# Two pairs per loop turn on TensorE in the attention stage of a fused two-block kernel

## The reference, cut to what matters

```python
s = jnp.einsum('bhrcd,bhrjkd->bhrcjk', qg, kg) + bias[None]
s = jnp.where(col_mask[:, None, :], s, -jnp.inf)
p = jax.nn.softmax(s.reshape(B, NA_HEADS, rows, GRID_W, kh * GRID_W), axis=-1).reshape(s.shape)
o = jnp.einsum('bhrcjk,bhrjkd->bhrcd', p, vg)
na_out = neighbourhood_attention(na_q, na_k, na_v, rpb) * jax.nn.silu(na_z)
...
return jnp.concatenate([na_out, ml_out], axis=-1) @ w_out
```

## Time and profile before

| what | value |
|---|---|
| median of 3 runs | 1884.34 us (1883.26 to 1884.55) |
| span of the profiled execution | 1883.3 us |
| granted TensorE clock, mean | 0.999 |
| PE busy | 1865.6 us, 99% of the span |
| DVE, ACT, POOL busy | 982.4, 618.3, 552.5 us (52%, 33%, 29%) |
| gate of pair 1 to the end of the last values matmuls | 1451.3 to 1628.4 us |

### The profile page before, as it was taken

The page is one execution under the profiler, slowest core; times in us unless marked ns, Lnnn a source line. Parts: engine busy times, 40 slices in busy tenths (PEclk is TensorE's granted clock), DMA queues, the critical chain, the costliest instruction groups (busy, mean ns, idle before and its releaser), DMA issues.

```text
span 1883.3 us, 26698 instructions
## 1 busy us (share of the span) xinstructions
PE 1865.6 (99%) x10035; PEld 1540.4 (82%) x10035; DVE 982.4 (52%) x2117; ACT 618.3 (33%) x1317; POOL 552.5 (29%) x925
## 2 busy tenths in 40 slices
PE   9999999999999999999999999999999999999998
PEld 8888878888888888888888787888887777788886
DVE  6556565775666433114777322223213777776665
ACT  7321111233444432101222202221114667655552
POOL 2112222233642222110110000222314777544442
PEclk9999999999999999999999999999999999999999
DMA  6223142366897745312221123665563776867663
GB/s 197 95 79 119 62 128 81 104 184 235 306 266 252 235 168 162 101 50 84 74 78 68 53 62 116 211 211 171 168 220 105 243 232 224 271 219 241 230 229 112
DMA packets 236365, 303.55 MB, mean 161 GB/s; under 512 B 41414, under 2 KB 161126, under 8 KB 236204
## 3 DMA queue, kind: packets, MB, share of 16 engines
q1 hardware_dynamic: 205724, 215.84, 37.4%
q0 software_dynamic: 23600, 77.61, 11.4%
q10 hardware_dynamic: 6912, 8.39, 1.2%
HBM read 194.71 MB, written 107.54 MB: 160 GB/s over the span
## 4 chain that ended last, share of the span: by engine, by line
PE 94%; DVE 2%; DMA 2%; issue 1%; ACT 1%; POOL 0%; SPq 0%; POOLq 0%; DVEq 0%; ACTq 0%
PE banks L145 25%; PE banks L147 25%; PE banks L146 25%; PE banks L2106 3%; PE banks L2069 3%; PE banks L2088 3%; PE banks L2704 2%; PE banks L2706 1%; PE banks L2397 1%; DMA iraw<-in_w_in 1%; PE banks L2089 1%; PE banks L2674 1%; PE banks L234 1%; PE banks L1109 1%; PE banks L1741 0%
## 5 line engine op out<-in xcount | busy, mean ns | idle before, releaser
L145 PE MATMUL banks<-hT,wu 128*128 128x512 f32 (+1 forms) x528 | 204.6, 387 | 1.1 <-DVE wu L512 0.6
L147 PE MATMUL banks<-hT,wu 128*128 128x512 f32 (+1 forms) x528 | 202.3, 383 | 0.0
L146 PE MATMUL banks<-hT,wu 128*128 128x512 f32 (+1 forms) x528 | 202.2, 383 | 0.0
L145 PE MATMUL banks<-iT,wub 128*128 128x512 f32 x384 | 151.2, 394 | 0.0
L145 PE MATMUL banks<-iT,wua 128*128 128x512 f32 x384 | 150.8, 393 | 0.0
L145 PE MATMUL banks<-wub,iT 128*128 128x512 f32 x384 | 150.6, 392 | 0.0
L147 PE MATMUL banks<-iT,wub 128*128 128x512 f32 x384 | 149.7, 390 | 0.0
L147 PE MATMUL banks<-iT,wua 128*128 128x512 f32 x384 | 149.5, 389 | 0.0
L146 PE MATMUL banks<-wub,iT 128*128 128x512 f32 x384 | 149.5, 389 | 0.0
L147 PE MATMUL banks<-wub,iT 128*128 128x512 f32 x384 | 149.5, 389 | 0.0
L146 PE MATMUL banks<-iT,wua 128*128 128x512 f32 x384 | 149.5, 389 | 0.0
(11 more groups left out here) (293 smaller groups left out, 4116.3 us busy)
## 6 DMA issues: line engine op xcount, KB each, us to landing
iraw<-in_w_in SPq DMA_DIRECT2D x36, 512.0 KB, 4.4
wa<-in_w_ada SPq DMA_DIRECT2D x48, 256.0 KB
yT<-sg POOLq DMA_DIRECT2D x32, 256.0 KB, 3.1
oraw<-yT SPq DMA_DIRECT2D x32, 256.0 KB, 4.8
xr<-in_x SPq DMA_DIRECT2D x16, 512.0 KB, 4.4
h<-h POOLq DMA_DIRECT2D x16, 512.0 KB, 4.3
hT<-tr POOLq DMA_DIRECT2D x16, 512.0 KB, 5.1
tws<-wg SPq DMA_DIRECT2D x16, 512.0 KB, 5.1
```

Source lines behind the costliest of these rows:

```text
L145: e.matmul(ps, lh, rh, start=first, stop=False)
L146: e.matmul(ps, lh, rl, start=False, stop=False)
L147: return e.matmul(ps, ll, rh, start=False, stop=last)
```

## The change

PE's loop and DVE's loop take steps of two (p = 0, 2, ..., 66). With q = p-2, an even pair, a turn of PE's loop is now: turn(q); scores(q+3) and scores(q+4) together; the tail's early work; turn(q+1); values(q-1) and values(q) together. A turn of DVE's loop is: invert(q+1), lower(q+2), copy(q); invert(q+2), lower(q+3), copy(q+1); then gate(q-1) and gate(q). ACT, POOL and SP keep their loops. The values of even and odd pairs go to two banks up to pair 53; from pair 54 all go to one, since the tail's scores need the other. The tail's first scores move from p = 57 to p = 58 and wait for gate 53 (`o_out.ge(54)`); its first numerators move from p = 63 to p = 64. The bodies of the turn, the values, the copy and the gate become functions with the same waits and instructions, but that the values wait for the last pair of their own bank.

```diff
-        self.pS, self.pT, self.pO = self.last[0:4], self.last[4:6], self.last[6]
+        self.pS, self.pT = self.last[0:4], self.last[4:6]
+
+        self.pO = [self.last[7] if q % 2 and q < 54 else self.last[6] for q in range(self.NP)]
...
     def dve(self, e, w, tail):
-        for p in range(self.NP + 3):
-            q = p - 1
-            if 1 <= q < self.NP:
-                self.invert(e, w, q)
-            if 2 <= p < self.NP:
-                self.lower(e, w, p)
-            tail.between_dve(e, w, p)
...
+        for p in range(0, self.NP + 3, 2):
+            for x in range(2):
+                if 1 <= p + x - 1 < self.NP:
+                    self.invert(e, w, p + x - 1)
+                if 2 <= p + x < self.NP:
+                    self.lower(e, w, p + x)
+                tail.between_dve(e, w, p + x)
+                self.copied(e, w, p + x - 2)
+            for x in range(2):
+                self.weighed(e, w, p + x - 3)
+                tail.early_dve(e, w, p + x)
...
+    def product(self, e, w, q):
+
+        if 0 <= q < self.NP:
+            hp, _, a = self.pairs[q]
+            nb, g0 = self.blocks(q), self.window(q)[0] // 4
+            w.wait_ge(*self.pt_dve.ge(q + 1))
+            w.wait_ge(*self.pt_act.ge(q + 1))
+            w.wait_ge(*self.vm_in[hp % 2].ge(2 * (hp // 2 + 1)))
+            w.wait_ge(*self.v_in[q % 4].ge(q // 4 + 1))
+            before = max((x for x in range(q) if self.pO[x] is self.pO[q]), default=None)
+            if before is not None:
+                w.wait_ge(*self.o_out.ge(before + 1))
...
     def pe(self, e, w, tail):
         w.wait_ge(*self.proj.row_step.ge(48))
-        for p in range(self.NP + 3):
-            if 1 <= p and p + 1 < self.NP:
-                self.scores(e, w, p + 1)
...
+        for p in range(0, self.NP + 3, 2):
+            self.turn(e, w, p - 2)
+            for x in (p + 1, p + 2):
+                if 2 <= x < self.NP:
+                    self.scores(e, w, x)
             tail.early_pe(e, w, p)
+            self.turn(e, w, p - 1)
+            self.product(e, w, p - 3)
+            self.product(e, w, p - 2)
...
     def early_pe(self, e, w, p):
-        if p == 57:
-
-            w.wait_ge(*self.att.proj.row_step.ge(48))
+        if p == 58:
+
+            w.wait_ge(*self.att.o_out.ge(54))
             self.scores(e, w, 0)
-        if p == 63:
+        if p == 64:
 
             w.wait_ge(*self.att.s_out.ge(128))
             self.numerators(e, w, 0)
-        if p == 64:
             self.scores(e, w, 1)
             self.product_n(e, w, 0, 0)
```

More of the change, by code:

```diff
@@ L1976, in invert @@
         e.reciprocal(self.st[:, 2 * q:2 * q + 2, 2], self.st[:, 2 * q:2 * q + 2, 1]).then_inc(*self.inverse.inc())
-    def dve(self, e, w, tail):
-        for p in range(self.NP + 3):
-            q = p - 1
-            if 1 <= q < self.NP:
-                self.invert(e, w, q)
-            if 2 <= p < self.NP:
-                self.lower(e, w, p)
-            tail.between_dve(e, w, p)
[L1986 to L2005, removed]
@@ new lines, in copied, with weighed @@
+    def copied(self, e, w, q):
+        if 0 <= q < self.NP:
+            n, N = 2 * q, (self.blocks(q) + 1) * P
+            w.wait_ge(*self.pt_full.ge(n + 1))
+            if q >= 2:
+                w.wait_ge(*self.o_full.ge(q - 1))
+            e.tensor_copy(self.ptr[n % 4][:, 0:N], self.pT[0][:, 0:N]).then_inc(*self.pt_dve.inc())
+    def weighed(self, e, w, q):
+        if 0 <= q < self.NP:
+            hp, i, a = self.pairs[q]
+            c0 = 32 * a
+            y = self.yr[q // 2 % 2]
+            z = self.zr[hp % 2][:].rearrange("p (r c) -> p r c", c=64)[:, 4 * i:4 * i + 4, c0:c0 + 32]
+            w.wait_ge(*self.o_full.ge(q + 1))
+            w.wait_ge(*self.z_in[hp % 2].ge(2 * (hp // 2 + 1)))
+            if q >= 4:
+                w.wait_ge(*self.y_st[q // 2 % 2].ge(q // 4))
+            e.tensor_tensor(y[:].rearrange("p (r c) -> p r c", c=64)[:, :, c0:c0 + 32],
+                            self.pO[q][:, 0:P].rearrange("p (r c) -> p r c", c=32), z, ALU.mult).then_inc(*self.o_out.inc())
@@ L2071, in scores, with turn @@
         t.then_inc(*self.s_full.inc())
+    def turn(self, e, w, q):
+        if 0 <= q < self.NP:
+            nb = self.blocks(q)
+            for x in range(2):
+                n = 2 * q + x
+                probs = self.pr[n % 8]
+                w.wait_ge(*self.scaled.ge(2 * n + 2))
+                if q >= 1:
+                    w.wait_ge(*(self.pt_act if x else self.pt_dve).ge(q))
+                for j in range(nb):
+                    e.transpose(self.pT[x][:, j * P:(j + 1) * P], probs[:, 160 * j:160 * j + P], self.ident[:])
+                e.transpose(self.pT[x][0:32 * nb, nb * P:(nb + 1) * P], self.er[n % 8][:, 0:32 * nb], self.ident[:]).then_inc(*self.pt_full.inc())
@@ new lines, in product @@
+    def product(self, e, w, q):
+        if 0 <= q < self.NP:
+            hp, _, a = self.pairs[q]
[7 more added lines that the diff above has]
+                w.wait_ge(*self.o_out.ge(before + 1))
+            for j in range(nb + 1):
+                for hh in range(2):
+                    d = slice(64 * hh, 64 * hh + 64)
+                    r = slice(0, P) if j < nb else slice(0, 32 * nb)
+                    v = self.vm[hp % 2][:, g0 + j, a, d] if j < nb else self.vr[q % 4][r, d]
+                    t = e.matmul(self.pO[q][d, 0:P], v, self.ptr[(2 * q + hh) % 4][r, j * P:(j + 1) * P], start=(j == 0), stop=(j == nb))
+            t.then_inc(*self.o_full.inc())
```

## The result

The changed kernel takes 1960.6 us (median of 4 runs, 1959.15 to 1965.29) against 1884.13 us: 1.040 times the time before, 95% interval 1.039 to 1.042. It is slower, as forecast, and the loop that was forecast is there, but it is slower by 76 us where the text said 53. The time lies 9 us above the forecast's own range (1924 to 1952) and 6 us above the wider one (1905 to 1955).

What follows compares the result with a forecast made beforehand. PE was taken to bound the kernel before, a loop over ACT's store after the change. The span 1883.3 + 52 + 1 + 2.4 - 2.4 = 1936.3 gave a median of 1937 us; own range 1924 to 1952, wider 1905 to 1955.

Steps and rivals of the forecast that it cites:

- the loop that was forecast: From gate(q-3) through ACT's store, exponentials and copy, then PE and DVE, to gate(q-1): 7.65 us per two pairs against 5.82.
- part 1: PE in attention: grouped scores and values drain less, saving 0.35 us in two pairs, about -10 us in all.
- Rival A: Drains alone count, the gates' new place holds nobody up: 1878 us, or 1874 without the one bank; chance 0.08.
- part 2: DVE's later gates delay ACT's store and the exponentials behind it, so two mid pairs cost 1.83 us more.
- The term that was least sure, from gate to exponential: In ACT's list, gate's end through the store's issue to the next exponential: 0.41 us, bounds 0.14 to 0.67.
- part 3: The hold comes in 30 double turns between gates 1 and 61, mean excess 1.74 us, 52 us in all.
- the tail's exponentials: Tail exponentials at p = 55, 57 and 59 in ACT's list, where ACT has little room: +1 us.
- head and end: Gate 1 comes later, +2.4 us; less is left behind gate 61, -2.4 us; the two cancel.
- rival C: PE's repeated stands bring the clock to 0.5, doubling PE's terms on the loop: +123, about 2060 us; chance 0.04.
- Rival B: Part of the loop is hidden, giving a period of 6.0 to 6.9 us: 1888 to 1916 us; chance 0.08.
- part 4: One bank from pair 54 hides in PE's stand; otherwise about 1 us at each of pairs 56, 58, 60 and 62.

Runs made afterwards that it cites:

- run 1: Changed kernel with ACT's wait for the gate and the store of y one step later in ACT's loop: 1900.56 us, 1.008 times the kernel before.
- run 8: Changed kernel with the store of y one step later in ACT's loop and three y buffers instead of two: 1895.57 us, 1.005 times the kernel before.
- run 9: Kernel before with only PE's loop changed, scores of two pairs together, turns and values still alternated: 1882.19 us against 1885.05, 0.998 times.
- run 2: Changed kernel with DVE doing the first of the two gates ahead of the odd pair's copy: 1924.37 us, 1.020 times the kernel before.
- run 6: Changed kernel with PE's loop back in the order of the kernel before, DVE's new order kept: 1908.7 us, 1.012 times the kernel before.
- run 4: Changed kernel with two extra wide matmuls on PE in each even turn, overwritten afterwards, filling its wait: 1943.33 us, 1.031 times the kernel before.
- run 3: Changed kernel with the first head's transposes done five times in even turns, filling PE's wait: 1943.22 us, 1.031 times the kernel before.
- run 7: Changed kernel with both the store of y one step later and the first gate ahead of the copy, two y buffers: 1895.36 us, 1.005 times.
- run 5: Changed kernel with DVE's loop back in the order of the kernel before, PE's grouping kept: 1942.38 us, 1.030 times the kernel before.

## Why the prediction was right in its way and wrong in its size

**What PE saves (part 1).** The scores of two pairs take 1.52 in one run, as forecast. The values save less: in the timeline of the changed kernel the first of two steps starts at 1531.56 and the second at 1532.48, 0.92 against 1.02, so 0.10, not 0.15. The saving was real but bought little: runs 1 and 8 show mid double turns of 5.63 to 5.78, not 5.47, and no gain over the middle of attention. Rival A (1874 to 1878) would not have come about even with the store moved. The page "TensorEngine Tiling (Array Packing)" of the Trainium skill, Key Properties, on the drain at a change of mode, still agrees with the 1.52 and the 0.92; by it alone the time would have been 1874, and the least that any run reached is the 1882 of run 9.

**The new order of the gates (part 2).** Right, and shown: the loop is there in the timeline, with 7.71 against 7.65; taking the store out of it removes it (run 1), shortening one term shortens it by that term (run 2), and it stands without PE's part (run 6). The term that was least sure, from gate to exponential, was taken at 0.41 and is 0.40.

**How often (part 3).** Thirty times, as the list of waits counts. The sum said 53 us over the span; with the clock held up, run 4's span of 1940.7 us makes it 57.4. The 25 double turns from gate 1 to gate 51 take 184.9 us in run 4 against 139.4: 1.82 more each where 1.74 was taken, which is 2 of the 4 us. The other 2 are in the last five: 12.8 more where the sum had 9.7 with the tail's exponentials (head and end give 0.8 of it back). Most of it is a slip in the sum, which took 2.4 us off behind gate 61 for tail work that now comes ahead of that gate, and added it nowhere. The matmuls of the tail that ran from 1621.46 to 1625.20 before, behind the values of pair 61, run from 1695.46 to 1699.22 in the changed kernel, ahead of them. In run 4 the double turn that ends at gate 61 takes 12.26 us where before it took 8.29, 4.0 more and not 1.74; from gate 61 to gate 63 it is 4.11 against 6.65.

**The step that failed** is the clock. The forecast's sum has no term for it: it stands only in rival C, as a fall in all thirty double turns, "so about 2060 us", with a chance of 0.04. It was treated as all or nothing and put outside the forecast. In fact the clock fell in 13 of 30 double turns for part of each, and each of those took 1.5 us more: 19 us, which with the 57 of the loop and the last pairs makes the 76. The forecast had itself said that PE would stand still for 2.2 us in each double turn (1.9 was measured), and that no stretch of the old trace shows such stands; still its own range ended at 1952. Runs 3 and 4 settle it: the same loop, PE's wait filled, no fall of the clock, 17 us less. Without the clock's part the forecast would have been right, 1943 against 1937.

The page "TensorE: Matmul & The Clock Gate" of the Trainium skill, Why this matters for your kernels, warns of idle gaps between bursts of matmuls. The 0.82 of the second double turn above agrees with it in kind, but the gaps that it warns of are longer than any wait of the changed kernel in attention, so the page alone would not have given this fall.

Rival B's bounds are a little off as well: 0.18 to 1.08 us in 30 double turns give 1890 to 1917, not 1888 to 1916. Nothing hangs on it.

**At nothing (part 4).** The row of the one bank, 5.0 us in five waits, stands in the changed kernel too, with the same numbers. At pairs 56, 58 and 60 PE waits 1.15 us for the gate there, and then 0.67, 0.67 and 0.53 for ACT's copy where it was 1.9: these waits hid in PE's stand, as said. At pair 62 the wait is 1.02 us, and no stand follows. In run 1 the same row is part of what the last ten pairs lose; it is the price that the text named, "about 1 us at each of pairs 56, 58, 60 and 62". What part 4 did not name is that a store now has one double turn to land where it had three pairs. In the changed kernel, at 7.7 us, no wait came of it; at 5.8 it did (run 1), and three buffers took it away (run 8).

**What stays open:** why the clock falls in one double turn and not in the next of the same kind; what in the last ten pairs of runs 1, 7 and 8 costs how much (one bank, the tail's moved work); and why the loads of `v` come late in run 9.

## What to carry to other kernels

When the order of one engine follows another's, look at what else waits for the steps that move: here a store's wait, in a third engine's list that nobody edited, turned a late gate into a hold on the exponentials behind it. Walk the loop from one such wait back to itself, through every list on the way, and add it up. That gave the period to 1% here and to 2% in run 6; in run 5, where the walk left out ACT, the sum was 0.4 us or more too short. A list of waits names what ended last, not always what released, so check against the starts. And where the sum says that PE will stand still again and again, count the clock in as a cost in part of the turns, not as an unlikely case of its own.

## What the runs showed of the hardware that was not expected

With PE waiting up to 1.9 us in each 7.7 us, the granted clock fell to its lower level, 1.2 GHz, 13 times in 249 us, the first time right behind the first such wait. In run 5, whose matmuls waited up to 1.4 us, it fell 8 times. With waits mostly up to 1.2 us (run 2) or 0.9 us (run 6) it didn't fall between gate 1 and gate 61; in run 2 it fell once just behind, at 1666.0 us. Run 1 had one fall in this stretch, during its one wait of 2.9 us. No boundary follows from this. Extra transposes kept the clock up as well as extra matmuls did (runs 3 and 4).
